# A causal convolution of width 31, split into its even and odd outputs on TensorE

## The reference

```
h = rms_norm(x, norm_g);  p = h @ w_in            # (N, T, 3456), split into 10 parts
a = a_val * sigmoid(a_gate)                       # group A: GLU, 384 channels
a_conv = causal depthwise conv(a, width 31) + a_conv_b
y_a = silu(layer_norm(a_conv, a_ln_g, a_ln_b)) * silu(a_z)
y_b = b_b * conv3(b_c * b_h) * silu(b_z)          # group B: 384 channels
y_c = c_u * (W_s @ layer_norm(c_v) + b) * silu(c_z)   # group C: 256, in chunks of 128
x = x + concat(y_a, y_b, y_c) @ w_out             # width 1024
```

## Time and profile before

| | |
|---|---|
| median of 3 runs | 620.64 us (620.28 to 621.94) |
| the profiled execution | 620.5 us, span of its slowest core 618.9 us |
| spans of the 8 cores | 607.9 to 618.9 us |
| TensorE busy | 589.0 us, 95% (4405 matmuls) |
| VectorE busy | 409.1 us, 66% |
| ScalarE busy | 259.5 us, 42% |
| GpSimd busy | 111.9 us, 18% |
| DMA | 89.43 MB, mean 144 GB/s |

### The profile page before, as it was taken

One profiled execution on the slowest core, in us unless ns is written; L12 is line 12 of the kernel. 1 busy time (PEld: TensorE's weight loads), 2 busy tenths in 40 slices (PEclk: granted clock), 3 DMA queues, 4 the chain that ended last, 5 costly groups with the idle time before them and its releaser, 6 DMA issues.

```text
span 618.9 us, 11365 instructions; the slowest of 8 cores (607.9 to 618.9 us)
## 1 busy us (share of the span) xinstructions
PE 589.0 (95%) x4405; PEld 323.4 (52%) x4430; DVE 409.1 (66%) x737; ACT 259.5 (42%) x445; POOL 111.9 (18%) x166
## 2 busy tenths in 40 slices
PE   7799999999999999999998998999998899999995
PEld 3535545555556656555643544545554555655552
DVE  2275974383868646675870893879278966956985
ACT  3445623042605724450651414642246265244462
POOL 4500510040113003000620600132003202200201
PEclk9799999999999999999999899999999999999999
DMA  8999789955892395489799998754473617515202
GB/s 188 162 140 216 108 98 191 213 143 121 187 218 44 53 178 162 96 226 193 201 126 233 187 165 152 189 152 130 110 175 123 134 35 220 155 49 99 103 2 102
DMA packets 77750, 89.43 MB, mean 144 GB/s; under 512 B 21888, under 2 KB 66624, under 8 KB 77696
## 3 DMA queue, kind: packets, MB, share of 16 engines
q1 hardware_dynamic: 55152, 64.97, 40.3%
q0 software_dynamic: 18176, 19.24, 25.3%
q10 hardware_dynamic: 4368, 4.49, 3.5%
HBM read 79.85 MB, written 30.52 MB: 178 GB/s over the span
## 4 chain that ended last, share of the span: by engine, by line
PE 68%; DVE 10%; DMA 9%; SPq 4%; ACT 3%; issue 3%; POOL 2%; DVEq 0%; ACTq 0%; POOLq 0%
PE pb L454 61%; PE pb L455 5%; DMA xr<-x_scr 3%; SPq L444 2%; DVE xr L422 2%; SPq L633 2%; DMA xr<-x_in 2%; ACT tmp L413 2%; DMA A<-as_scr 2%; DVE h_tm L434 2%; DMA h_scr<-h_tm 2%; DVE xr L434 1%; DVE nv L430 1%; PE pb L615 1%; DVE tmp L434 1%
## 5 line engine op out<-in xcount | busy, mean ns | idle before, releaser
L454 PE MATMUL pb<-h_fm,w_in_sb 128*128 128x384 bf16 (+3 forms) x2020 | 366.5, 340 | 10.3 <-ACT h_fm L413 7.2
L454 PEld LDWEIGHTS pb<-h_fm,w_in_sb 128*128 128x128 bf16 x2032 | 196.5, 98 | 169.1 <-issue 5.8
L413 ACT ACTIVATE tmp<-pb 128x384 f32<-128x384 f32 (+2 forms) x110 | 57.0, 519 | 216.8 <-PE pb L454 215.2
L454 PE MATMUL pb<-w_out_sb,mix 128*128 128x512 bf16 (+1 forms) x532 | 115.6, 383 | 5.3 <-ACT tmp L413 3.0
L454 PEld LDWEIGHTS pb<-w_out_sb,mix 128*128 128x128 bf16 (+1 forms) x544 | 52.0, 99 | 67.7 <-ACT tmp L413 3.1
L413 ACT ACTIVATE tmp<-xr 128x1024 bf16<-128x1024 f32 (+2 forms) x52 | 53.8, 1035 | 68.0 <-DVE xr L422 39.6
L422 DVE TENSOR_TENSOR xr<-pb,xr 128x512 f32<-128x512 f32 (+1 forms) x72 | 47.9, 688 | 45.1 <-PE pb L454 44.8
L558 POOL TENSOR_SCALAR rstd<-ss 128x1 f32<-128x1 f32 (+1 forms) x46 | 23.9, 520 | 239.0 <-ACT tmp L413 238.0
L455 PE MATMUL pb<-A,W 128*32 128x384 bf16 (+2 forms) x1152 | 47.0, 313 | 2.1 <-DMA A<-as_scr 2.1
L434 DVE SCALAR_TENSOR_TENSOR h_tm<-xr,rstd,ng_b 128x1024 bf16<-128x1024 f32 (+1 forms) x30 | 39.0, 1303 | 8.7 <-POOL rstd L559 5.7
L434 DVE SCALAR_TENSOR_TENSOR tmp<-z_ext,pc,tmp 128x384 f32<-128x384 bf16 (+1 forms) x60 | 37.9, 639 | 8.1 <-ACT tmp L413 7.9
(11 more groups left out here) (99 smaller groups left out, 448.7 us busy)
## 6 DMA issues: line engine op xcount, KB each, us to landing
A<-a_scr SPq DMA_DIRECT2D x96, 103.0 KB, 4.3
w_in_sb<-w_in POOLq DMA_DIRECT2D x17, 512.0 KB, 22.0
xr<-x_in SPq DMA_DIRECT2D x16, 512.0 KB, 9.0
x_scr<-xr SPq DMA_DIRECT2D x16, 512.0 KB, 8.8
xr<-x_scr SPq DMA_DIRECT2D x16, 512.0 KB, 8.0
y_o<-xr SPq DMA_DIRECT2D x15, 512.0 KB, 3.5
w_out_sb<-w_out POOLq DMA_DIRECT2D x4, 1024.0 KB, 18.2
w_in_scr<-w_in POOLq DMA_DIRECT2D x7, 512.0 KB, 14.8
```

The costliest lines, as they stand in the source:

```text
L413: S.add("act", lambda e: e.activation(out=out, in_=in_, func=func, **kw), reads=reads, writes=writes, cost=170 + 0.833 * free_size(out) + ...
L454: return lambda e: e.matmul(out, lhsT, rhs, start=start, stop=stop)
```

## The change

The convolution is computed for even and odd outputs apart. With x split into pairs, and filters H0 (even taps) and H1 (odd taps), three half-rate filters of 16 taps replace four: one filter works on the sums of neighbouring tokens (`S4`, made by `pair_sum`), the other two on A4 at every second element, with weights from which the shared filter is subtracted. The shared filter's result `u` (its own PSUM bank, half the columns) is added to both halves of `v` when they are evacuated into `y`. A4 now holds shifts of 0, 2, 4, 6 tokens. `y` lives in `h_fm` of the block's own parity (in `xr` slots 8 and 9 for the first block), the conv's banks are released after the evacuation, and the norm subtracts the mean from `y` straight out of the statistics' bank. The new tiles take SBUF, and `xr` and `tmp` have fewer slots.

```diff
-NX = 12
+NX = 10
-NTMP = 7
+NTMP = 6
-        W4 = sb("W4", [128, 12, 8, 32], BF16)
+        W4 = sb("W4", [128, 12, 12, 32], BF16)
+        S4 = sb("S4", [128, NA4, 4, NHA // 2], BF16)
...
         def params_comp(l, after=()):
+            wf = wc4[:].rearrange("p (b f m) -> p b f m", f=3, m=4)
+            S.add("dve", lambda e: e.tensor_tensor(
+                out=wf[:, :, 1:3, :], in0=wf[:, :, 1:3, :], in1=wf[:, :, 0:1, :].broadcast_to([128, 12, 2, 4]),
+                op=ALU.subtract), reads=["wc4"], writes=["wc4"], cost=190, after=after)
...
+        def pair_sum(s, w, eng):
+            tt(S4[:, s, :, 0:w], A4[:, s, :, 0:2 * w:2], A4[:, s, :, 1:2 * w:2], ALU.add, a4_keys(s), [("s4", s)], eng=eng)
...
         def a4_load(l, blk, c, smp, after=()):
...
+                pair_sum(s, ncol // 2, "dve")
             else:
-                ncol = blk.np + 28
+                ncol = blk.np + 24
...
+                pair_sum(s, ncol // 2, "pool")
...
         def a4_shift(c):
...
+            pair_sum(s, (NMAX + 24) // 2, "dve")
...
+        def conv(l, blk, c, s, banks, smp):
             np_, n = blk.np, blk.n
+            vb_, ub_, uo = banks
             mms = []
...
+            for f in range(3):
+                for m in range(4):
+                    for q in range(4):
+                        lo, o = (4 * m, np_ // 2) if f == 0 else (8 * m + 2 - f, np_)
+                        bank, base, st = (ub_, uo, 1) if f == 0 else (vb_, (f - 1) * (n // 2), 2)
+                        T = (S4 if f == 0 else A4)[:, s, q, :]
...
+                            rhs = T[:, lo:lo + o:st]
+                            out = pbank[bank][32 * q:32 * q + 32, base:base + np_ // 2]
+                        mms.append(mm(out, W4[:, 4 * c + q, 4 * f + m, :], rhs, m == 0, m == 3, (0, 32 * q)))
...
+        def conv_evac(l, blk, c, banks, par):
...
-            act(f[d], P[c], AF.Square, [pk(banks[c]), "pc"], [fk[d]], bias=colA(l, c, 0))
-            if c == 0:
-                act(f[2], P[0], AF.Identity, [pk(banks[0]), "bsum"], [fk[2]], bias=bsum[:, l:l + 1])
...
+            act(us, pbank[u_][:, uo:uo + h], AF.Identity, [pk(u_), "pc"], [tk], bias=colA(l, c, 0))
+            tt(ys[c].rearrange("p (k s) -> p s k", s=2), pbank[v_][:, 0:n].rearrange("p (s k) -> p s k", s=2),
+               us.unsqueeze(1).broadcast_to([128, 2, h]), ALU.add, [pk(v_), tk] + (hk if c else []),
+               [("yk", c)] + ([] if c else hk))
+            act(f[d], ys[c], AF.Square, [("yk", c)] + hk, [fk[d]])
             if c == 1:
...
+                tt(f[2], ys[0], ys[1], ALU.add, [("yk", 0), ("yk", 1)] + hk, [fk[2]], eng="pool")
+                tt(f[0], f[0], f[1], ALU.add, [fk[0], fk[1]], [fk[0]], eng="pool")
...
-            act(mean, pbank[b1][:, 0:n], AF.Copy, [pk(b1)], ["mean"] + hk, scale=1.0 / WA)
...
+                stt(ys[c], pbank[b1][:, 0:blk.n], -1.0 / WA, ys[c], ALU.mult, ALU.add, [pk(b1), ("yk", c)] + hk, [("yk", c)])
```

More of the change, by code:

```diff
@@ new lines, in conv, with y_region @@
+            pe(mms, ["w4", ("s4", s)] + a4_keys(s), [pk(vb_), pk(ub_)], 12 * max(46, (0 if smp else np_) / 4.8 + 4))
+        cs = {}
+        def y_region(l, blk, par):
+            if l == 0 and blk.first:
+                v = [xr[:, 8, 0:512], xr[:, 8, 512:1024], xr[:, 9, 0:512], xr[:, 9, 512:1024]]
+                return [a[:, 0:blk.n] for a in v], XK(8) + XK(9)
+            v = h_fm[:, par, :].bitcast(F32)
+            return ([v[:, 512 * i:512 * i + blk.n] for i in range(4)],
+                    [("hfm", par, k, hv) for k in range(8) for hv in (0, 1)] + [("hfj", par, j) for j in range(4)])
@@ L877, in stage_stats @@
                    n / 2.4)
[L878 to L884, removed]
-            act(mean, pbank[b1][:, 0:n], AF.Copy, [pk(b1)], ["mean"] + hk, scale=1.0 / WA)
+            ys, hk = cs["y"]
+            vb = ys[3]
+            cs["b1"] = b1
             act(vb, pbank[b1][:, 0:n], AF.Square, [pk(b1)] + hk, ["vb"], scale=1.0 / WA)
@@ L1073, in build_program, with convs @@
         A_half(1, 1)
-        def convs(l, blk, a4, cbanks, cs):
-            for c in cs:
-                conv(l, blk, c, a4[c], cbanks[c], False)
+        def convs(l, blk, a4, cb, cl, par):
+            for c in cl:
+                if not blk.smp:
+                    cb[c] = (balloc(), balloc(), 0)
+                elif c == 1:
+                    cb[c] = (balloc(), cb[0][1], NMAX // 2)
+                else:
+                    cb[c] = (balloc(), balloc(), 0)
+                conv(l, blk, c, a4[c], cb[c], False)
                 if blk.smp:
@@ L1100, in cv @@
         def cv(c):
-            pcb[c] = balloc()
-            convs(l, blk, a4, pcb, [c])
+            convs(l, blk, a4, pcb, [c], 0)
         def ld():
@@ L1190, in build_program @@
             if tail:
-                pcb = [balloc() for _ in range(3)]
-                convs(l, blk, a4, pcb, range(3))
+                convs(l, blk, a4, pcb, range(3), 1 - cur["par"])
             for c in range(3):
@@ L1214, in build_program @@
             if not tail:
-                pcb = [balloc() for _ in range(3)]
-                convs(l, blk, a4, pcb, [0])
+                par = cur["par"]
+                convs(l, blk, a4, pcb, [0], par)
                 if pt:
```

138 lines of the change are left out of this document (67 added, 71 removed).

## The result

The changed kernel takes 667.1 us (median of 4 runs, 662.5 to 669.2) against 620.5 us of the kernel before (4 runs, 620.3 to 621.9): 1.074 times as long, 95% interval 1.068 to 1.079. The prediction was 628 us in a range of 613 to 640; the sign came out as forecast, the size lies far outside. The profiled execution took 667.0 us, its slowest core 665.5.

The account below looks back on a forecast made before the run. TensorE, busy 95% of the span, was taken as the bound. 620.5 - 9.9 + 1.25 + 1.5 + 3.0 + 0.5 + 10.0 + 1.0 = 627.9, so 628 us; range for 8 in 10: 613 to 640.

Parts of the forecast that it names:

- the price of nothing for what stands behind a pair sum: GpSimd's queue: reciprocal roots and weight loads behind a pair sum awaiting A4 have many us in a plain block; no cost.
- Position 24: Sample tile's load in layer 1 block 0 waits for an old tile's store, stalling TensorE: +10.0 us (2 to 15).
- rival (a): Sample tile's load is hidden because the old tile's store issues before the weights crowd the queues: 617 us, chance 0.24.
- Positions 10 and 27: Two other loads into slots of the previous block still come just in time: 0.5 us together (0 to 6).
- Lock: VectorE and GpSimd block each other, x adds and z products reading PSUM stay free: 1 us over the run (0 to 5).
- First block: Longer weight build and first pair sum on VectorE stand ahead of conv 0: +1.5 us (0 to 4).
- Evacuation and sample convs: Evacuation chain covered by next block's projections, no cost; sample convs' pair sum and longer evacuation +3.0 us (0 to 7).
- Convs: TensorE's convs in 12 half-width steps instead of 8: 1.115 us at 384 columns, 1.435 at 512, -9.9 us in all.
- rival (c): Convs' reads of A4 at every second element run at half speed: +20 us, 648 us, chance 0.06.
- rival (d): A floor on matmul start-to-start times eats the convs' gain: 638 us, chance 0.02.
- rival (b): The VectorE-GpSimd lock makes VectorE late, mostly at 60 to 84 us and after sample blocks: +7, 635 us, chance 0.10.

Follow-up runs that it names:

- the sums over W4: Kernel before plus 27 unused pair sums on GpSimd, reading W4 columns that always lie in SBUF instead of A4 tiles: 627.0 us, 1.007.
- the roots first: Kernel before with ten x slots, the sample tile's norm in layer 1 put after stage_CV's reciprocal roots: 626.8 us, 1.011.
- both suspects: Kernel before with tiles at position modulo 10 and 27 unused pair sums of A4 on GpSimd: 660.0 us, 1.058.
- ten slots: Kernel before with tiles put at their position modulo 10 instead of 12, nothing else: 635.0 us, 1.025.
- the change without sums: Changed kernel without pair sums, first filter run over even then odd elements of A4, 16 steps a conv: 650.3 us, 1.048.
- the change with late sums: Changed kernel with GpSimd's pair sums moved behind the norms (last block: ahead of stage_CV): 664.8 us, 1.071.
- the kernel with two repairs: Changed kernel without pair sums, eleven slots, second tile's adds back on VectorE, weight build after the third a_t product: 638.3 us, 1.023.
- Without pair sums and slots: Changed kernel without pair sums, 16 steps a conv, with eleven x slots instead of ten: 639.0 us, 1.033.
- the later statistics: Kernel without pair sums, eleven slots, two repairs, plus statistics after a sample block one projection pair later: 629.9 us, 1.015.

## Why the prediction was wrong

**The step that failed** is the price of nothing for what stands behind a pair sum: "they have many us in a plain block". Of the 41.2 us of the median core, 15.9 arise in blocks 3 and 4 of layer 0, although their convs gained 0.7 to 0.8 us each time, so that the price there is some 17 us. The work was sized right (GpSimd is busy for 69.7 us more, 70 forecast). That it is the waiting and not the work, the sums over W4 show (4.2 against 27.9 us). What is true of a plain block is not true of the one whose A4 loads run among layer 1's weights. The rows for it were there before: those A4 tiles landed only just ahead of their convs. I asked when the convs need A4, and never when GpSimd would stand before it, and for whom. In the sample blocks VectorE stands before A4 in the same way, 16.9 us ahead of three of the six sums (list of waits); what that costs was not tried by itself.

**Position 24**: right in cause and place, with the price off. 10.0 us were forecast (2 to 15), 15.7 measured alone (12 to 19 by the interval). The Square that waits for the load starts at 377.07 where 374 was worked out. With the roots first it costs 7.1 us (4.8 to 9.3), through ScalarE, as the prediction had allowed; the other 8.6 come from GpSimd's queue, the same mistake a second time: `rstdc` stands behind the root of the late tile. In the changed kernel the stretch shows only 5.7 us, with both suspects in the kernel before 13.4. SyncE and GpSimd show one difference, here in the change and then in the kernel before with ten slots:

```profile
378.01 4.61 SPq L444 DMA_DIRECT2D x_scr<-xr  x2
378.49 1.88 POOL L444 DMA_DIRECT2D w_out_sb<-w_out  x2
382.72 0.46 SPq L444 DMA_DIRECT2D xr<-x_scr  x1
...
357.56 1.85 POOL L444 DMA_DIRECT2D w_out_sb<-w_out  x2 [1.61 <-PE pb L454]
359.18 2.88 SPq L444 DMA_DIRECT2D x_scr<-xr  x2
369.24 0.46 SPq L444 DMA_DIRECT2D xr<-x_scr  x1
```

In the change the store of the old tile leaves ahead of the load of w_out on all eight cores and lands after 2.6 to 4.6 us; in the kernels "ten slots" and "both" of the table it leaves behind that load and takes 6.7 to 10.0. So the tile's own load leaves 41 to 46 us after the last conv of layer 0 instead of 48 to 54, and TensorE waits 4.9 to 8.6 us for `nv` instead of 10.2 to 15.8. This is the order that rival (a) asked for; but the tile's load then takes 8.7 to 9.8 us itself, and the wait stays. In the change without sums, too, the two cores whose store takes 3.1 and 5.1 us wait 4.7 and 5.9, and the six with 9.0 to 10.9 wait 11.5 to 13.2. That the order is the cause is read from these times and was not tried by itself.

**Positions 10 and 27** (0.5, up to 6): nothing in the kernel before with ten slots. In the changed kernel the load at position 27 waits for the store of an output tile, and TensorE stands 3.91 us before the last transpose into h_fm at 476.62 (1.5 to 5.9 on seven of the eight cores). The slot alone does not do it: the load waits for such a store in the kernel before with ten slots, in that with both suspects, in the change with late sums and in that without sums too, and none of these has the wait on any core. What adds to it stays open.

**Lock** (1.0, 0 to 5): 4.2 us with prompt sums, in the bounds, with the rest of GpSimd's work in it. Its price by itself stays open: late, the same sums cost 13.5 us more on GpSimd than on VectorE, but they also take longer there. The products of `zs_ext`, which were held up, read no PSUM: the z products were not all free, as the prediction had it.

**First block** (1.5, 0 to 4): 2.8 us with the gain of its convs in it (1.25 by the prediction's 0.42 each), so some 4. The build takes 4.96 us and stands ahead of the third a_t, for which TensorE waits 2.42 us (0.46 before); the eight matmuls behind that wait then take 3.28 us instead of 1.90, at a granted clock of 0.50 from 41.5 to 43 us (1.00 in the kernel before). The clock after the wait was the part not counted; with the build behind the third a_t, in the kernel with two repairs, the stretch is 3.9 us shorter.

**Evacuation and sample convs** (0 and 3.0, up to 7): small in the plain blocks, wrong in the sample blocks. The cover I named, the next block's projections, is used up between the sample convs. Without pair sums and slots it still cost some 10 us over both layers (2.5, 2.7 and 4.8 in the table, with the 16 steps of these convs in it); moving GpSimd's two adds took away 0.9 of that and the later statistics another 2.6, so that 6.5 us stay open. The ratio fell from 1.033 over 1.023 to 1.015 with block 0's gain in it.

**Convs** (-9.9): right. 1.13 and 1.34 us against 1.115 and 1.435 worked out. A sample conv takes 0.50 us to the next start (488.30 to 488.80), a little over the 0.30 to 0.46 that were counted as nothing against 0.35. Reads at every second element cost nothing that these times show, which ends rival (c). As for rival (d): in a sample conv of this kernel the 16 matmuls over S start at 482.31 and those over A at 482.44, some 8 ns apart on average, so the floor of the Trainium skill (TensorE: Matmul & The Clock Gate, section "Wait — 56ns, not 53.3ns?"), about 25 ns, does not hold for four column groups side by side. Within one column group the starts are some 32 ns apart, above that floor. Rival (a) fell, and rival (b) by its mechanism: VectorE was late, but through GpSimd's queue.

**Together**: both suspects cost 36 us in the kernel before. The change without them, whose convs of 16 steps gain nothing, costs 20 (1.033). Less the 9.9 us of the convs this makes 46 to 47, and the change lost 46; that it fits so well is in part luck, since delays need not add.

## What to carry to other kernels

Work on an engine that is 18% busy is not free: ask what each new instruction waits for and who stands behind it in that queue, in the stretch where its input is latest and not in a plain one. An instruction that waits for a transfer belongs behind all that others need from its engine, or on the engine that needs the transfer anyway. And a change that pays 0.3 us a time must be costed where its cover is thin: at the first block, at the odd block, at the border of layers.

## What was not expected of the hardware

A VectorE copy of two elements can take as long as the GpSimd instructions beside it: 649 ns on average with late pair sums, 4.67 us at the worst, to the end of three pair sums in a row, where it takes 0.17 us undisturbed. On these rows the length of the GpSimd instructions beside it, and not its own size, sets its time. And the cores of one program differ by 30 us once waits for transfers lie on the path (the wait for h_tm in block 4 is 2.6 us on one core and 15.4 on another); the time is that of the slowest.
